# Loads, stores and clears placed differently in a two-layer hybrid decoder: four gate/up buffers, rows out by tile, projections started row tile first

## The chip, the cores and the metric

One Trainium2 chip, one of its cores. The time is the device time of one launch in microseconds, as the median of several runs. Before the change it is 4256.31 us (3 runs, 4256.29 to 4258.72). TensorE (PE) multiplies, VectorE (DVE), ScalarE (ACT) and GpSimd (POOL) do the elementwise work, and SyncE (SP) issues most of the transfers.

## The reference, cut to what matters

1024 tokens of width 1024 go through two layers, all in float32.

```python
for layer in range(2):
    h = rmsnorm(x, norm_mix[layer])
    if layer == 0: x = x + pool_mixer(h, ...)        # windowed means minus the row, four 256x256 matrices, a scale
    else:          x = x + nsa_mixer(h, ...)         # 16 heads, 4 kv heads: compressed, selected and window attention
    h = rmsnorm(x, norm_ffn[layer])
    if layer == 0: x = x + (silu(h @ wg) * (h @ wu)) @ wd    # 1024 -> 3584 -> 1024
    else:          x = x + moe(h, ...)               # router picks 2 of 8 experts of the same shape for each token
    if layer == 0: shared = build_shared_kv(x, ...)  # keys and values of all three branches, from x after layer 0
```

## The kernel before, in words

The kernel is one program of stages, each a block of five instruction streams (one for each engine). A stage has semaphores of its own, which `phase_semaphores` clears at its end, with a barrier of all engines. The stages in order: `pool_mixer`, `swiglu_jobs` for the dense channel mixer ("ffn"), `project_heads` ("kvq"), `compress_keys` ("cmp"), `attend` ("att"), `project_out`, `route`, and `swiglu_jobs` again for the experts ("moe"). Within a stage the order on each engine is the order of the code, and semaphores tie the engines together.

Float32 products are made of three passes: each operand is split into a high part (a cast to the fast 32-bit format, on ACT) and the low rest (a subtraction, on DVE), and PE adds high by high, high by low and low by high.

**`swiglu_jobs`** runs a list of jobs. A job is one expert's weights with up to 384 rows. Its width is one of six (128 to 384), and the jobs run from the widest down. In this data the experts make eight jobs: 384, 352, 320, three of 256, 224 and 128 rows. The dense mixer makes two jobs of 512 rows. A job has MT = 28 gate/up tiles (1 MB of weights each) and NG = 14 down groups (1 MB each). The raw gate/up weights land in two buffers `gu_raw`. ACT makes `gu_hi` of a tile (`split`, L221 to L225), DVE makes `gu_lo` (L306 to L309), and only then may SP load the tile after the next into that buffer (`load_gate_up` waits for `s_gu_lo`, L157). For widths over 128 PE holds the weights still and streams the rows (`gate_up`, L414). For width 128 it is the other way round (`rows_by_weights`, L430), and the hidden rows are transposed behind it (`turn_hidden`, L442). After two tiles comes one down group (`down`, L454), whose sums DVE adds into `yacc` (`add_y`, L335).

At a job's end POOL waits for the last of these sums (L209), copies the row numbers of the job (L2381), issues one adding indirect transfer for each row tile (L2387), pads the count of three with tiny transfers to `spare` (L2391), waits until all have landed (L211), and clears `yacc` for the next job (L204). DVE waits for the clearing (L364) in front of its second tile of the next job. PE transposes the next job's rows before the last down group. They were gathered by POOL (L2373) at the start of the job before. For the first job of the experts nothing precedes: the three gathers are issued while SP already loads gate/up tiles 0 and 1 and down group 0.

**The dense mixer** stores its 512x1024 result `yacc` in one transfer (L2320) after the last sum. **`pool_mixer`** ends with five DVE copies of bias rows out of PSUM (L725) and behind them the last normalised row tile (L699), which SP stores, and then the bias rows (L623).

**`project_heads`** multiplies the eight row tiles by five chunks of 512 columns. ACT does `weight_hi` (L947), `square_x` (L940) and `transposed_x` (L964), and issues the loads of row tiles (`load_x`, L931). DVE does `add_x`, `normed_x`, `low_x`, `weight_lo`. PE transposes row tile i+1 before it multiplies row tile i. Before the change the first four weight slices stand ahead of row tile 0 on ACT and DVE, and `multiply` waits for all eight low slices. **`attend`** begins on SP with the queries of row tile 0 (`load_q`), the keys of tile 0, the constants and values, the queries of tile 1, the keys of tile 1.

## Time and profile before

| what | value |
|---|---|
| median of the runs | 4256.31 us |
| the profiled execution: its own time | 4260.62 us |
| its span, first to last instruction | 4258.1 us |
| mean granted clock of TensorE | 0.969 |
| PE busy | 4030.5 us, 95% |
| DVE busy | 2364.7 us, 56% |
| ACT busy | 1630.4 us, 38% |
| transfers, mean over the span | 139 GB/s |
| gate/up load of 1 MB, issue to landing, median of 226 | 4.8 us |
| granted clock around the first gathers, 2080 to 2101 | 0.53 |

Times in the rows below are microseconds from the start of the span. A matmul's printed duration holds part of its pipeline, so the distance between the starts of two matmuls is the better measure of what one costs. A granted clock of 1.00 is 2.4 GHz, 0.50 is 1.2 GHz.

### The profile page before, as it was taken

How to read it: one execution, taken by the hardware profiler on the slowest of the kernel's cores; microseconds unless marked ns; L12 is line 12 of the kernel's file. 1: busy time of each engine (PE TensorE's matmuls, PEld its weight loads, DVE VectorE, ACT ScalarE, POOL GpSimd, SP SyncE). 2: the span in 40 equal slices, each digit the busy share in tenths (PEclk: the TensorE clock that was granted, in tenths of full speed). 3: DMA queues.
4: the chain of work that ended last, by engine and by line, in shares of the span. 5: the costliest groups of instructions: out<-in, count | busy, mean ns of one | idle time of the engine just before them, and what ended most of it. 6: DMA issues, size and time to landing. Idle time of an engine off the chain costs nothing.

```text
span 4258.1 us, 63421 instructions
## 1 busy us (share of the span) xinstructions
PE 4030.5 (95%) x23002; PEld 3477.4 (82%) x23002; DVE 2364.7 (56%) x3487; ACT 1630.4 (38%) x2255; POOL 425.4 (10%) x433
## 2 busy tenths in 40 slices
PE   7999999997997899998599999999999999999987
PEld 6888888886886555557599999999989999999976
DVE  4444444445443776643455555555566666666677
ACT  3222222222332676672232332333334444444445
POOL 2000000000231243330100010010010101001010
PEclk9999999998998899999699999999999999999998
DMA  5222232223544211005333343344455555555566
GB/s 215 99 100 99 97 128 89 108 99 144 167 137 149 72 43 37 17 18 180 135 132 118 138 151 125 142 153 148 148 175 188 198 190 179 209 185 194 198 239 220
DMA packets 153287, 592.17 MB, mean 139 GB/s; under 512 B 26768, under 2 KB 54800, under 8 KB 112915
## 3 DMA queue, kind: packets, MB, share of 16 engines
q1 hardware_dynamic: 138788, 545.92, 35.6%
q0 software_dynamic: 10288, 35.14, 2.9%
q10 hardware_dynamic: 4080, 9.44, 0.6%
q8 instruction: 73, 1.20, 0.1%
q14 instruction: 58, 0.48, 0.0%
HBM read 533.66 MB, written 57.83 MB: 139 GB/s over the span
## 4 chain that ended last, share of the span: by engine, by line
PE 44%; DMA 3%; DVE 1%; issue 1%; POOL 1%; ACT 1%; POOLq 0%; DVEq 0%; SPq 0%; ACTq 0%
PE moe_ps L424 9%; PE moe_ps L425 9%; PE moe_ps L426 9%; PE moe_ps L466 5%; PE moe_ps L467 5%; PE moe_ps L468 5%; DMA moe_gu_raw<-in_moe_wgu 2%; DVE moe_gu_lo L308 1%; DMA spare<-ident 1%; PE moe_ps L405 1%; ACT moe_gu_hi L225 0%; DMA out_x<-moe_yacc,job_to 0%; POOL moe_yacc L204 0%; DVE moe_yacc L343 0%; DMA moe_stage<-h_moe,moe_ids 0%
## 5 line engine op out<-in xcount | busy, mean ns | idle before, releaser
L424 PE MATMUL moe_ps<-moe_ht_hi,moe_gu_hi 128*128 128x256 f32 (+4 forms) x3136 | 941.5, 300 | 10.2 <-DVE moe_gu_lo L308 8.6
L426 PE MATMUL moe_ps<-moe_ht_hi,moe_gu_lo 128*128 128x256 f32 (+4 forms) x3136 | 940.2, 300 | 0.0
L425 PE MATMUL moe_ps<-moe_ht_lo,moe_gu_hi 128*128 128x256 f32 (+4 forms) x3136 | 939.8, 300 | 0.0
L225 ACT CAST moe_gu_hi<-moe_gu_raw 128x2048 fp32r<-128x2048 f32 x226 | 430.6, 1905 | 553.1 <-PE moe_ps L426 484.4
L308 DVE TENSOR_TENSOR moe_gu_lo<-moe_gu_raw,moe_gu_hi 128x2048 fp32r<-128x2048 f32 x226 | 517.4, 2289 | 183.7 <-ACT moe_gu_hi L225 183.4
L424 PEld LDWEIGHTS moe_ps<-moe_ht_hi,moe_gu_hi 128*128 128x128 f32 x3136 | 599.7, 191 | 14.9 <-DVE moe_gu_lo L308 9.7
L425 PEld LDWEIGHTS moe_ps<-moe_ht_lo,moe_gu_hi 128*128 128x128 f32 x3136 | 600.4, 191 | 3.5
L426 PEld LDWEIGHTS moe_ps<-moe_ht_hi,moe_gu_lo 128*128 128x128 f32 x3136 | 599.3, 191 | 0.0
L343 DVE SCALAR_TENSOR_TENSOR moe_yacc<-moe_ps,job_weights,moe_yacc 128x512 f32<-128x512 f32 x504 | 374.8, 750 | 340.0 <-PE moe_ps L468 340.0
L466 PE MATMUL moe_ps<-moe_wd_hi,moe_hid_hi 128*128 128x512 f32 x1008 | 396.2, 393 | 0.0
L467 PE MATMUL moe_ps<-moe_wd_lo,moe_hid_hi 128*128 128x512 f32 x1008 | 393.9, 391 | 0.0
L468 PE MATMUL moe_ps<-moe_wd_hi,moe_hid_lo 128*128 128x512 f32 x1008 | 393.5, 390 | 0.0
L424 PE MATMUL ffn_ps<-ffn_ht_hi,ffn_gu_hi 128*128 128x512 f32 x896 | 349.9, 391 | 1.9 <-DVE ffn_ht_lo L304 1.9
L426 PE MATMUL ffn_ps<-ffn_ht_hi,ffn_gu_lo 128*128 128x512 f32 x896 | 349.8, 390 | 0.0
L425 PE MATMUL ffn_ps<-ffn_ht_lo,ffn_gu_hi 128*128 128x512 f32 x896 | 349.6, 390 | 0.0
L346 DVE TENSOR_TENSOR ffn_yacc<-ffn_yacc,ffn_ps 128x512 f32<-128x512 f32 x224 | 153.6, 688 | 255.3 <-PE ffn_ps L468 255.0
L250 ACT CAST moe_hid_hi<-moe_hid 128x256 fp32r<-128x256 f32 (+4 forms) x196 | 85.0, 434 | 528.0 <-DVE moe_hid L323 528.0
L333 DVE TENSOR_TENSOR moe_wd_lo<-moe_wd_raw,moe_wd_hi 128x2048 fp32r<-128x2048 f32 x112 | 255.9, 2285 | 0.0
L323 DVE TENSOR_TENSOR moe_hid<-moe_act_gate,moe_ps 128x256 f32<-128x256 f32 (+5 forms) x224 | 96.9, 433 | 285.9 <-PE moe_ps L426 255.7
L468 PEld LDWEIGHTS moe_ps<-moe_wd_hi,moe_hid_lo 128*128 128x128 f32 x1008 | 189.4, 188 | 40.1
L466 PEld LDWEIGHTS moe_ps<-moe_wd_hi,moe_hid_hi 128*128 128x128 f32 x1008 | 190.0, 188 | 37.0 <-DVE moe_yacc L343 1.1
L467 PEld LDWEIGHTS moe_ps<-moe_wd_lo,moe_hid_hi 128*128 128x128 f32 x1008 | 189.7, 188 | 35.5
(355 smaller groups left out, 6490.7 us busy)
## 6 DMA issues: line engine op xcount, KB each, us to landing
moe_gu_raw<-in_moe_wgu SPq DMA_DIRECT2D x226, 1024.0 KB, 4.8
moe_wd_raw<-in_moe_wd SPq DMA_DIRECT2D x112, 1024.0 KB, 6.7
first_gu<-in_ffn_wgu SPq DMA_DIRECT2D x58, 1024.0 KB, 4.8
ffn_wd_raw<-in_ffn_wd SPq DMA_DIRECT2D x28, 1024.0 KB, 6.8
att_qt<-qt SPq DMA_DIRECT2D x8, 1024.0 KB, 4.9
kt<-kt_rows SPq DMA_DIRECT2D x8, 1024.0 KB, 6.9
shared<-in_w_kvq SPq DMA_DIRECT2D x5, 1024.0 KB, 7.8
kvq_raw<-in_w_kvq SPq DMA_DIRECT2D x5, 1024.0 KB, 7.7
```

The costliest lines, as they stand in the source:

```text
L225: act.copy(gu_hi[s][:, :, :, :].rearrange("p a k c -> p (a k c)"), gu_raw[s][:, :]).then_inc(s_gu_hi, 1)
L308: dve.tensor_tensor(gu_lo[s][:, :, :, :].rearrange("p a k c -> p (a k c)"), gu_raw[s][:, :], gu_hi[s][:, :, :, :].rearrange("p a k c -> p ...
L323: dve.tensor_tensor(hid[s][:, 0:W], act_gate[s][:, 0:W], gate_ps[s][:, W:2 * W] if W == P else up_ps[s][:, 0:W], ALU.mult).then_inc(s_hid, 1)
L333: dve.tensor_tensor(wd_lo[b][:, :, :], wd_raw[b][:, :, :], wd_hi[b][:, :, :], ALU.subtract).then_inc(s_wd_lo, 1)
L343: dve.scalar_tensor_tensor(out=part, in0=y_ps[u % 4][:, :], scalar=row_weights[1][:, t:t + 1], in1=part, op0=ALU.mult, op1=ALU.add).then_i ...
L346: dve.tensor_tensor(part, part, y_ps[u % 4][:, :], ALU.add).then_inc(s_yadded, unit)
L424: pe.matmul(out[:, 0:W], gu_hi[s][:, half, k, :], ht_hi[:, k, 0:W], start=(k == 0), stop=False)
L425: pe.matmul(out[:, 0:W], gu_hi[s][:, half, k, :], ht_lo[:, k, 0:W], start=False, stop=False)
L426: last = pe.matmul(out[:, 0:W], gu_lo[s][:, half, k, :], ht_hi[:, k, 0:W], start=False, stop=(k == KT - 1))
L466: pe.matmul(out, hid_hi[b][:, a, rows], wd_hi[b][:, a, cols], start=(a == 0), stop=False)
L467: pe.matmul(out, hid_hi[b][:, a, rows], wd_lo[b][:, a, cols], start=False, stop=False)
L468: last = pe.matmul(out, hid_lo[b][:, a, rows], wd_hi[b][:, a, cols], start=False, stop=(a == GROUP - 1))
```

## The change

It makes these edits; the diff is cut to its core.

- Experts: four gate/up buffers in place of two. The dense mixer keeps two (`RING` is the number). The order of loads on SP stays: one down group, two gate/up tiles, but the tiles are two further ahead.
- Experts' start: SP loads tile 0, waits until the gathered rows of the first job have landed, and only then loads tiles 1 to 3 and the first down group.
- At a job's end POOL copies the row numbers first and waits for the sums of one row tile at a time (`tile_done`), issuing each tile's transfer behind its own wait. The dense mixer stores four transfers of one row tile each in place of one.
- DVE's wait for the cleared `yacc` stands in `add_y`, where `yacc` is used.
- `pool_mixer`: the five copies of bias rows run on ACT, at its end. DVE's last `normed_mid` no longer stands behind them.
- `project_heads`: row tile 0 is squared, normalised and transposed ahead of the weights, `load_x(2)` stands right behind `transposed_x(0)`, the first multiplication is done in two halves with the transposes of row tile 1 between, and `multiply` waits for each weight slice by itself.
- `compress_keys`: SP loads the queries of row tiles 0 and 1 here, into the memory of a buffer that `zrow` no longer needs. `attend` begins with the keys.

```diff
-            stage, gu_raw = sb("stage", [P, CAP, D]), [sb(f"gu_raw{s}", [P, 2 * D]) for s in range(2)]
+            stage, gu_raw = sb("stage", [P, CAP, D]), [sb(f"gu_raw{r}", [P, 2 * D]) for r in range(4)]
...
+        def gu_load_count(j, n, r):
+            return j * (16 // RING * MT) + (n - r) * (16 // RING) + 16
...
-            def load_gate_up(ws, j, n, s):
-                sp.wait_ge(s_gu_lo, j * MT + n + 1)
+            def load_gate_up(ws, j, n, r, first=False):
+                if not first:
+                    sp.wait_ge(s_gu_lo, j * MT + n + (3 - RING))
...
-                for s in range(2):
-                    load_gate_up(first, 0, s, s)
+                load_gate_up(first, 0, 0, 0, first=True)
+                sp.wait_ge(s_rows, 16 * CAP)
+                for r in range(1, RING):
+                    load_gate_up(first, 0, r, r, first=True)
...
-                            load_gate_up(ws, j, it * 4 + (2 * b + 2 + s), s)
+                            load_gate_up(ws, j, it * 4 + (2 * b + RING + s), (2 * b + s) % RING)
+                for q in range(IN_JOB - IN_JOB % 2, NG):
+                    load_down(ws, j, q, q % 2)
+                    if q == IN_JOB:
+                        following = source(j + 1)
+                    for s in range(2):
+                        n = 2 * q + RING + s
+                        load_gate_up(ws if n < MT else following, j, n, n % RING)
...
-                pool.wait_ge(s_yadded, j * 24 * NG + (24 + 24 * NG))
-                put(pool, j, base, yacc, s_stored, per_height)
+                def tile_done(t, tiles):
+                    unit = 12 // tiles
+                    pool.wait_ge(s_yadded, j * 24 * NG + (24 * NG + unit * (2 * t + 2)))
+                    pool.sem_inc(s_store_seen, 1)
+                put(pool, j, base, yacc, s_stored, per_height, tile_done)
...
                     def add_y(q):
+                        dve.wait_ge(s_zeroed, j + 1)
...
                     wdlo(0, 0)
-                    dve.wait_ge(s_zeroed, j + 1)
...
+            for n, (a, b) in enumerate(spans):                       # pool_mixer, ACT, after square_mid(TILES - 1)
+                act.wait_ge(s_vec_mm, n + 1)
+                act.copy(vec[:, a:b], vec_ps[n][0:N_HEADS, 0:b - a]).then_inc(s_vec_made, 1)
...
             load_x(1)                                                # project_heads, ACT
+            square_x(0)
             act.wait_ge(s_gain, 16)
             for k in range(HK):
                 weight_hi(0, k)
-            square_x(0)
+            transposed_x(0)
+            load_x(2)
+            square_x(1)
...
             add_x(0)                                                 # project_heads, DVE
+            normed_x(0)
             dve.wait_ge(s_gain, 16)
             for k in range(HK):
                 weight_lo(0, k)
-            normed_x(0)
+            add_x(1)
+            low_x(0)
+            normed_x(1)
...
             transpose_x(0)                                           # project_heads, PE
-            for n in range(STEPS):
+            multiply(0, half=0)
+            transpose_x(1)
+            multiply(0, half=1)
+            for n in range(1, STEPS):
...
+            for z in range(2):                                       # compress_keys, SP
+                sp.wait_ge(s_tr, (z + 1) * N_KV)
+                load_q(sp, z)
...
-            load_q(0)                                                # attend, SP
             load_keys(0)
...
-            load_q(1)
             load_keys(1)
...
-            pool.dma_start(y_ffn.rearrange("(s p) d -> p s d", p=P)[:, bass.ds(base, DENSE_W // P), :], yacc[:, :, :]).then_inc(s_stored, 16)
+            tiles = DENSE_W // P
+            for t in range(tiles):
+                tile_done(t, tiles)
+                pool.dma_start(y_ffn[bass.ds((base + t) * P, P), :], yacc[:, t, :]).then_inc(s_stored, 16)
...
                 for t in range(tiles):
+                    tile_done(t, tiles)
                     pool.indirect_dma_start(out=out, out_offset=bass.IndirectOffsetOnAxis(ap=job_to[:, t:t + 1], axis=0),
```

## Rows read from the trace of the kernel before

**Rows 1.** Waits of PE over the span: total us, times, longest us.

```profile
PE moe_ps L405 <- DMA moe_stage<-h_moe,moe_ids: 24.3, 1, 24.3
...
PE moe_ps L447 <- DVE moe_hid L323: 19.8, 8, 6.2
...
PE moe_ps L424 <- DVE moe_gu_lo L308: 8.6, 4, 3.8
```

**Rows 2.** Waits in the 128-row job, 4076 to 4243.

```profile
ACT moe_gu_hi L225 <- DMA moe_gu_raw<-in_moe_wgu: 37.8, 21, 4.8
```

**Rows 3.** The 128-row job in time: start, duration, engine, line, operation, idle before.

```profile
4091.82 0.29 DVE L323 TENSOR_TENSOR moe_hid<-moe_act_gate,moe_ps 128x128 f32<-128x128 f32 x1 [4.96 <-POOL moe_yacc L204]
...
4097.06 2.28 DVE L333 TENSOR_TENSOR moe_wd_lo<-moe_wd_raw,moe_wd_hi 128x2048 fp32r<-128x2048 f32 x1
...
4229.18 2.29 DVE L333 TENSOR_TENSOR moe_wd_lo<-moe_wd_raw,moe_wd_hi 128x2048 fp32r<-128x2048 f32 x1
...
4167.58 0.28 PE L433 MATMUL moe_ps<-moe_gu_hi,moe_ht_hi 128*128 128x256 f32 x1
...
4176.48 0.28 PE L433 MATMUL moe_ps<-moe_gu_hi,moe_ht_hi 128*128 128x256 f32 x1
```

**Rows 4.** Stretches: PE, PEld, DVE, ACT, POOL busy; clock; transfers' share; GB/s.

```profile
4125.00:4150.00 25.00, 22.77 (x165) 20.99 (x163) 20.84 (x23) 14.00 (x17) 0.00 (x0) 1.00 0.80 305
...
3125.00:3130.00 5.00, 4.85 (x22) 4.85 (x23) 5.00 (x6) 2.70 (x3) 4.39 (x3) 0.50 0.71 265
...
3858.00:3864.00 6.00, 6.00 (x28) 6.00 (x29) 5.14 (x5) 2.74 (x4) 5.34 (x3) 0.50 0.80 292
```

**Rows 5.** The start of the first 256-row job: PE in time.

```profile
3120.99 0.28 PE L425 MATMUL moe_ps<-moe_ht_lo,moe_gu_hi 128*128 128x256 f32 x1
3121.11 0.28 PE L426 MATMUL moe_ps<-moe_ht_hi,moe_gu_lo 128*128 128x256 f32 x1
...
3125.95 0.42 PE L424 MATMUL moe_ps<-moe_ht_hi,moe_gu_hi 128*128 128x256 f32 x1
3126.16 0.42 PE L425 MATMUL moe_ps<-moe_ht_lo,moe_gu_hi 128*128 128x256 f32 x1
```

**Rows 6.** The first gathers: third one's landing; all gathers; packets of 2078 to 2100 by queue.

```profile
moe_stage<-h_moe,moe_ids POOLq DMA_INDIRECT x1, 12.2
...
DMA to landing us min/median/max: 4.2/9.7/12.9
...
q1 hardware_dynamic: 704, 4.19, 48.2%
q0 software_dynamic: 432, 1.57, 17.6%
```

**Rows 7.** The end of the dense mixer: POOL in time, then a stretch as in rows 4.

```profile
1018.24 0.76 POOL L2320 DMA_DIRECT2D y_ffn<-ffn_yacc  x1 [448.59 <-DVE ffn_yacc L346]
1027.19 0.10 POOL L892 MEMSET kvq_minus_half<- 128x8 f32 x1 [8.20 <-POOLq L41]
...
1020.00:1021.00 1.00, 0.00 (x0) 0.00 (x0) 0.00 (x0) 0.00 (x0) 0.00 (x0) 1.00 1.00 401
```

**Rows 8.** The start of the projections, in time; then the first store's landing.

```profile
1048.74 1.23 DVE L1040 TENSOR_TENSOR first_sum<-first_sum 128x1024 f32<-128x1024 f32 x1 [3.02 <-DMA first_sum<-y_ffn]
...
1040.53 0.34 ACTq L937 DMA_DIRECT2D first_sum<-x_mid  x1
...
x<-first_sum SPq DMA_DIRECT2D x1, 512.0 KB, 9.0
```

**Rows 9.** The start of the attention, in time.

```profile
1369.79 4.44 SPq L1476 DMA_DIRECT2D att_consts<-in_sel_const  x1
...
1378.38 0.75 DVE L1641 TENSOR_TENSOR shared<-att_s,cmpb 128x256 f32<-128x256 f32 x2 [13.45 <-DMA att_valid<-in_row_valid]
```

**Rows 10.** The end of the pool mixer: DVE in time.

```profile
72.12 2.46 DVE L725 COPY pool_vec<-pool_d 16x512 f32<-16x512 f32 x4
```

**Rows 11.** The end of the kernel: POOL in time.

```profile
4246.33 1.63 POOL L2387 DMA_INDIRECT out_x<-moe_yacc,job_to  x1 [1.89 <-issue]
```

More of the change, by code:

```diff
@@ L77, in swiglu_jobs @@
         else:
-            stage, gu_raw = sb("stage", [P, CAP, D]), [sb(f"gu_raw{s}", [P, 2 * D]) for s in range(2)]
-            s_gu_loaded = [sem(f"gu_loaded{s}") for s in range(2)]
+            stage, gu_raw = sb("stage", [P, CAP, D]), [sb(f"gu_raw{r}", [P, 2 * D]) for r in range(4)]
+            s_gu_loaded = [sem(f"gu_loaded{r}") for r in range(4)]
+        RING = len(gu_raw)
+        def gu_load_count(j, n, r):
+            return j * (16 // RING * MT) + (n - r) * (16 // RING) + 16
         ids = sb("ids", [P, CAP], mybir.dt.uint32)
@@ L257, in wdhi, with post_and_split @@
                         act.copy(wd_hi[b][:, :, :], wd_raw[b][:, :, :]).then_inc(s_wd_hi, 1)
-                    def post_and_split(m, q, s, b, first=False):
+                    def post_and_split(m, q, s, b, r, first=False):
                         silu(j * MT + m, s)
@@ L346, in add_y, with post_and_split @@
                                 dve.tensor_tensor(part, part, y_ps[u % 4][:, :], ALU.add).then_inc(s_yadded, unit)
-                    def post_and_split(m, s, b, first=False):
+                    def post_and_split(m, s, b, r, first=False):
                         product(j * MT + m, s)
@@ L1160, in transpose_x, with multiply @@
                 last.then_inc(s_t, 1)
-            def multiply(n):
+            def multiply(n, half=None):
                 c, i = divmod(n, TILES)
@@ L1171, in multiply @@
                 at_rows = slice(i * P, (i + 1) * P)
-                for k in range(KT):
+                for k in range(KT) if half is None else range(half * HK, half * HK + HK):
+                    if i == 0:
+                        pe.wait_ge(s_wlo, c * KT + k + 1)
                     pe.matmul(acc[n % 4][:, :], xt_hi[:, k, at_rows], w_hi[c % 2][:, k, :], start=(k == 0), stop=False)
@@ L1176, in multiply @@
                                      start=False, stop=(k == KT - 1))
-                last.then_inc(s_mm, 1)
+                if half != 0:
+                    last.then_inc(s_mm, 1)
             def transpose_heads(n):
@@ L1218, in _, with compress_keys @@
                 transpose_gates(half)
-def compress_keys(nc, zrow, first_w1, pos, w1, w2, kc_gain, ident, kct, vc):
+def compress_keys(nc, zrow, first_w1, pos, w1, w2, kc_gain, ident, kct, vc, load_q):
     NBL = 64
@@ L1402, in attend @@
         vs, vw = first_sum[:, :].rearrange("p (i n) -> p i n", i=TILES), sb("vw", [P, TILES, N_KV * DH])
-        qt = [sb(f"qt{s}", [P, N_HEADS, P], F32R) for s in range(2)]
         p_slc = [sb(f"p_slc{s}", [P, R, SEQ]) for s in range(2)]
@@ L1421, in attend @@
         o_ps = [ctx.enter_context(nc.psum_tensor(f"att_o{s}", [P, 512], F32)) for s in range(2)]
-        s_const, s_qt = sem("const"), [sem(f"qt{s}") for s in range(2)]
+        s_const = sem("const")
         s_kt, s_values = [sem(f"kt{s}") for s in range(2)], sem("values")
@@ L2331, in trunk, with load_q @@
             vc = sb(att, "vc", [P // 2, N_KV, DH])
+            w_lo1 = sb(att, "kvq_lo1", [P, KT, 512], F32R)
+            qt = [w_lo1[:, 4 * s:4 * s + 4, :].rearrange("p a (b t) -> p (a b) t", t=P) for s in range(2)]
+            s_q = [nc.alloc_semaphore(f"queries{s}") for s in range(2)]
+            def load_q(sp, i):
+                sp.dma_start(qt[i % 2].bitcast(F32), qt_dram[i * P:(i + 1) * P, :].rearrange("p (h t) -> p h t", t=P)
+                             ).then_inc(s_q[i % 2], 16)
             with ExitStack() as early:
                 raw = [shared[:, :].rearrange("p (k n) -> p k n", k=KT // 2), sb(early, "kvq_raw", [P, KT // 2, 512])[:, :, :]]
-                w_lo1 = sb(early, "kvq_lo1", [P, KT, 512], F32R)
                 zrow = [w_lo1[:, 4 * z:4 * z + 4, :].bitcast(F32).rearrange("p m (g l d) -> p m g l d", g=N_KV, l=2) for z in range(2)]
```

118 lines of the change are left out of this document (56 added, 62 removed).

## The prediction, written before the result was known

> **What bounds the kernel now.** I read the share of busy time first: PE works 95% of the span, so only what ends PE's idle time, or its time at half clock, can pay. The list of PE's waits [rows 1] then says where that is: 24.3 us for the first gathered expert rows, 19.8 us in the 128-row job for hidden rows that DVE makes late, 8.6 us at four job starts for `gu_lo`. The other places are the seams between stages, where PE waits for a new stage's first data. The reader is to see that all edits are at such places. In the long middle of every wide job PE has no wait, and nothing there changes.
>
> One stage is not bound by PE's own work: the last job, 128 rows wide. Its ACT waits 37.8 us for gate/up transfers in 21 pieces [rows 2]. From the second to the fourteenth low part of a down group it takes 4229.18 - 4097.06 = 132.1 us [rows 3], 12 steps of 11.01 us. A step is a pair of gate/up tiles and a down group. PE does one in 4176.48 - 4167.58 = 8.90 us where nothing holds it [rows 3]. DVE is busy 20.84 of 25 us there [rows 4], 0.83 of 11.01, so 9.2 us. PE and DVE are almost equal, and the transfers at 305 GB/s have 0.80 of the engines' time [rows 4]. A step moves three loads, 3.15 MB. At the 401 GB/s that a full stretch shows [rows 7] that is 7.8 us.
>
> **The sum, part by part,** against the profiled execution's own 4260.6 us, which is 4.3 us over the median. I subtract the same number from the median.
>
> *Four gate/up buffers.* Before, a tile's raw load may only start when the low part of the tile two before is made, and ACT then waits for its landing. With four, the load starts two tiles (some 9 us) earlier against the page's median of 4.8 us to land, so those 37.8 us go. What is late next is PE or DVE: the step is no shorter than 8.90, and DVE's 9.2 is a sum of durations that overlap a little. I take 9.2 us. 12 x (11.01 - 9.2) = 21.7 us. Bounds: 12 x (11.01 - 8.90) = 25.3 us, and 0 if transfers or SP's order keep the step. In wider jobs the buffers hide nothing: there PE waits for no load.
>
> *Clearing awaited at use.* DVE's second tile of a job waited for `yacc`. In the 128-row job that is 4.96 us [rows 3], and all behind it on DVE (the low parts of tile 3 and of down group 1) follows, so 4.9 us. In the three 256-row jobs and the 224-row job PE's waits for `gu_lo` [rows 1] go, 8.6 us. Two of these were long enough to be followed by half clock: 5 us behind 3125 and 6 us behind 3858 [rows 4]. A 256-column matmul starts every 0.12 us at full clock and every 0.21 at half [rows 5], so of 11 us some 0.43 is lost, 4.8 us. Together 18.3 us. The new wait is in front of the first `add_y`. It stands behind four gate/up tiles and a down group, over 25 us into the wide jobs. In the narrow one these are 4 x 3 + 2.7 us plus the start's waits, some 17 us from 4076, and the clearing was over at 4091.8, 15.7 us in [rows 3], with copying ahead making it 2 us earlier. So I cost it at nothing, with 3 us of cover. If that were gone, DVE's next splits would queue behind the wait, and PE behind them, each us one to one. That the cleared memory is written beside DVE's work costs nothing new, since POOL already issued such clears beside DVE.
>
> *Rows awaited before more weights.* The third gather took 12.2 us to land while 4.19 MB of weights moved beside 1.57 MB of rows [rows 6]. After the change only tile 0 (1.05 MB) competes, and 2.6 MB take 6.5 us from 2080.5, to 2087. The quickest gather of all landed in 4.2 us [rows 6], which from 2083.2 is 2087.4. I take that: 8.0 us. The bound on the low side is the median landing of 9.7 us: 2.5 us. Nothing waits behind SP's held queue: tile 1 is wanted 8 us after PE begins, and one load takes 4.8 us. The down group comes fourth, some 12 us after the rows, against 11 us plus 6.4 us of transposes before ACT asks for it. The Trainium skill (DMA: Bandwidth & Descriptors, Queues, rings and completion order) says that each transfer engine turns between its queues packet by packet. By that rule the 432 row packets would have met 432 of the 704 weight packets, 2.57 MB, and 4.1 MB at 401 GB/s put the landing near 2091, not 2095.4. The gain would be nearer 4 us, as part of the landing is then the gather's own. The trace does not agree fully, as the rows came last.
>
> *Stores by tile.* The dense result leaves in one 2 MB transfer issued at 1018.24, and the next stage starts at 1027.19 [rows 7]. The last tile alone is 0.5 MB, so three quarters of 5.2 us at 401 GB/s move ahead, under the last sums: 3.8 us, bounds 3.0 and 4.2. At a job's end in the experts each output transfer goes out earlier, hidden by PE's next tiles. Only at the kernel's end is it on the path, and there only because the row numbers are copied ahead of the wait: 1.89 us of issue [rows 11] become some 0.3. That is 1.8 us with the copy.
>
> *Projections.* Row tile 2's load was issued at 1040.53, landed for the sum at 1048.74, and from there each row tile takes 7.0 us, the time of its load and sum, to the end of the chunk. So the whole chunk moves with this load. After the change its issue waits for the first store, which landed 9.0 us behind its issue at 1029.3 [rows 8], so 1038.3, 2.2 us earlier. It then also has less traffic beside it (the second half of chunk 1 is issued later). I put its sum 4.0 us earlier. Bounds: 2.2, and 5.0 where it lands like the later ones, in 5.4 us.
>
> *Attention.* DVE's first work waits 13.45 us, to 1378.38, for the last small constant. The issue of the constants alone held SP for 4.44 us [rows 9], behind queries and keys. Without the queries in front, the keys' 1 MB lands 2.6 us sooner at 401 GB/s, or, if the queue stays held as long, only the 0.7 us of their issue is won. I take 2.5. In `compress_keys` the two query loads lie beside one weight load that is wanted 15 us later. They cost nothing, and if they delayed it, each us would count one to one.
>
> *Pool mixer.* Four copies take 2.46 us on DVE from 72.12 [rows 10], with the fifth 2.9 us in front of the last row tile. On ACT, idle there, they end at the same time or slightly later, and the last tile no longer follows them: 1.7 us of 1.3 to 1.9.
>
> *What it adds.* DVE's wait in each `add_y`, PE's per-slice waits, POOL's wait and count per tile: some 300 instructions, hidden but in the 128-row job and at the end. I take 1 us.
>
> Sum: 21.7 + 18.3 + 8.0 + 3.8 + 1.8 + 4.0 + 2.5 + 1.7 - 1.0 = 60.8 us. The profile would read 4199.8, the median **4195.5**.
>
> **The rivals.** *The narrow job stays at its transfers' pace.* SP still issues in one fixed order, and 0.80 of the transfer engines' time is used already. If latency under a fuller queue or SP's place in the order holds, the step stays near 11 us. The job then gains only the clearing, and the time is 4256.3 - 39.1 = 4217.2. Against it: the landings are under 8 us and would have 17. In between lie half gains, about 4206.
>
> *The gathers are slow by themselves.* The median of 27 gathers is 9.7 us [rows 6], though nearly all had weights beside them. Then 5.5 us are missing: 4201. By the Trainium skill's rule above (same section) it would be about 4199.
>
> *Half clock in the narrow job (the slower side).* Half clock followed waits of 3.76 and 2.4 us and not those of 1.1 and 1.3. If PE, once ahead of DVE, stood over 2.5 us in every step, a step would run at half clock. 48 matmuls of 256 columns cost 10.1 us instead of 5.8, and the rest doubles from 3.1, so about 16.3 us a step. 12 x (16.3 - 11.01) = 63 us more, and the time is 4256.3 - 39.1 + 63 = 4281. It decides from 15 us a step on (39.1 + 8.5 us over 12 steps, on top of 11.01). Against it: the stretch ran at 1.00 even with the transfer waits [rows 4], and these waits go.
>
> *The change doesn't do what it says* in one seam: a stage's first data lands late for another reason, say keys or the first stored row. Each is 2 to 4 us.
>
> **How the numbers follow.** The forecast with its seams as priced, narrow step 8.9 to 9.7 us: 0.62, with a range of its own of 4187 to 4205. The narrow job at its old pace or half way: 0.24, 4205 to 4221. Gathers slow or two seams failing with the narrow job right: 0.09, within 4198 to 4210. Half clock, or another loss over the whole gain: 0.03. Better than all bounds: 0.02. The range for 8 in 10 is 4186 to 4218: it takes in the best bounds (another 3.6 + 0.9 + 0.4 + 1.0 us, and some tail) and the old pace. A measurement of this kernel tells about 0.2%, 8.5 us, from no change. Faster by more: 0.95. Within it: 0.02. Slower: 0.03.
>
> **What would show it.** In the 128-row job ACT's waits for `moe_gu_raw` are near nothing and `moe_wd_lo` starts every 9.2 us. PE has no wait for `moe_gu_lo` at job starts, and no half clock at the first 256-row and the 224-row job. The first expert transposes start about 7 us after the first gather is issued instead of 15. The dense mixer's last issue and the next stage's first instruction are 5 us apart instead of 9. In the projections the first sum of row tile 2 comes 17 to 18 us into the stage, not 21.6. DVE's first work in the attention comes 7.4 us into the stage instead of 9.95. Wrong would be: a step still at 11 us with waits on DMA (first rival), a new wait of DVE for POOL's clearing in front of `add_y`, or w1 of the compression landing after PE wants it.

## The result, and the profile after

The changed kernel takes **4197.4 us** (median of 4 runs, 4194.9 to 4201.7) against 4256.3 before. The ratio is 0.9861, with a 95% interval of 0.9849 to 0.9874. The forecast was 4195.5, with 4186 to 4218 as its range. The profiled execution took 4201.67 us (span 4200.1, granted clock 0.973), so between the two profiled executions lie 58.0 us of span, where the sum had 60.8.

I cut both spans at the first instruction of each stage and read what each term became. Seams are measured as in the last part of the prediction.

| term of the sum | forecast | before to after, from rows | measured |
|---|---|---|---|
| four gate/up buffers | 21.7 | 12 steps of the narrow job: 132.1 to 110.7 | 21.4 |
| clearing awaited at use | 18.3 | jobs 3 to 7: 15.3 shorter; narrow job up to its second `wd_lo`: 20.2 to 15.2 | 20.3 |
| rows before more weights | 8.0 | experts' start to first `ht_hi`: 17.0 to 10.5 | 6.4 |
| stores by tile | 3.8 | last dense addition to next stage: 10.4 to 6.8 | 3.6 |
| tail | 1.8 | last `wd_lo` to the end: 28.9 to 27.4 | 1.5 |
| projections | 4.0 | stage: 295.0 to 293.8 | 1.2 |
| attention's first work | 2.5 | 9.9 to 6.9 | 3.1 |
| pool mixer | 1.7 | last scale to next stage: 9.45 to 7.75 | 1.7 |
| instructions added | -1.0 | nothing seen | 0 |
| elsewhere | 0 | pool mixer 1.9 shorter; dense mixer 2.1 longer, compression 0.1 longer, attention from its first work to the experts' start 0.9 longer | -1.3 |

The measured column gives 57.9. The row "elsewhere" is no effect of the change (last section).

PE's list of waits in the changed kernel, the answer to [rows 1] (line waited at, by whom, us in total, times, longest):

```profile
PE moe_ps L424 <- DMA moe_stage<-h_moe,moe_ids: 17.9, 1, 17.9
PE kvq_t L1186 <- DVE first_sum L1067: 16.7, 4, 11.3
...
PE moe_ps L466 <- DVE moe_hid L342: 4.7, 4, 1.6
```

24.3 became 17.9, 19.8 became 4.7 (the turning of hidden rows, now L466), and of the four waits for `gu_lo` 0.2 us are left. The projections' wait shows that a seam is left there.

The narrow job, low parts of down groups two, three and fourteen on DVE, the answer to [rows 3], and the windows (busy us of PE, PEld, DVE, ACT and POOL, then granted clock, DMA share, GB/s), the answer to [rows 4]:

```profile
4062.07 2.29 DVE L352 TENSOR_TENSOR moe_wd_lo<-moe_wd_raw,moe_wd_hi 128x2048 fp32r<-128x2048 f32 x1
4071.25 2.29 DVE L352 TENSOR_TENSOR moe_wd_lo<-moe_wd_raw,moe_wd_hi 128x2048 fp32r<-128x2048 f32 x1
...
4172.77 2.29 DVE L352 TENSOR_TENSOR moe_wd_lo<-moe_wd_raw,moe_wd_hi 128x2048 fp32r<-128x2048 f32 x1
```

```profile
4120.00:4145.00 25.00, 25.00 (x182) 23.39 (x181) 24.37 (x27) 17.01 (x21) 0.00 (x0) 1.00 0.90 340
```

(4172.77 - 4062.07) / 12 = 9.23 us a step. DVE is busy 24.37 of 25 us, so it is the bound, as forecast. The transfers went from 0.80 to 0.90 of the engines' time without holding anything. In this job ACT has no wait for a gate/up load any more.

The experts' start on POOL and PE (third gather's issue, first transposes), the answer to [rows 6], and the seam behind the dense mixer on POOL, the answer to [rows 7]:

```profile
2074.97 0.94 POOL L2412 DMA_INDIRECT moe_stage<-h_moe,moe_ids  x1 [0.30 <-issue]
```

```profile
2080.78 4.75 PE L424 MATMUL moe_ps<-ident,moe_stage 128*128 128x128 f32 x24 [17.92 <-DMA moe_stage<-h_moe,moe_ids]
```

```profile
1016.85 0.53 POOL L2352 DMA_DIRECT2D y_ffn<-ffn_yacc  x1 [2.18 <-DVE ffn_yacc L367]
1022.19 0.10 POOL L911 MEMSET kvq_minus_half<- 128x8 f32 x1 [4.81 <-POOLq L41]
```

The third gather lands 5.8 us behind its issue, not the forecast's 4.2. The last 0.5 MB store takes 5.3 us to the next stage's first instruction, where 2 MB took 8.95.

The projections on ACT and its queue (loads of row tiles 2 and 3, squares of tiles 1 and 2), and on DVE two low parts of weights and the sums, the answer to [rows 8]:

```profile
1032.65 0.33 ACTq L956 DMA_DIRECT2D first_sum<-x_mid  x1
1033.02 1.00 ACTq L957 DMA_DIRECT2D first_sum<-y_ffn  x1
1034.06 1.06 ACT L964 ACTIVATE kvq_work<-kvq_work 128x1024 f32<-128x1024 f32 x1 [4.52 <-issue]
...
1042.16 1.06 ACT L964 ACTIVATE first_sum<-first_sum 128x1024 f32<-128x1024 f32 x1 [3.27 <-DVE first_sum L1063]
1042.25 0.33 ACTq L956 DMA_DIRECT2D kvq_work<-x_mid  x1
```

```profile
1039.59 1.41 DVE L1076 SCALAR_TENSOR_TENSOR kvq_lo<-shared,kvq_gains,kvq_hi 128x512 fp32r<-128x512 f32 x2
1040.91 1.22 DVE L1063 TENSOR_TENSOR first_sum<-first_sum 128x1024 f32<-128x1024 f32 x1
...
1049.33 1.23 DVE L1063 TENSOR_TENSOR kvq_work<-kvq_work 128x1024 f32<-128x1024 f32 x1 [1.70 <-DMA kvq_work<-y_ffn]
```

The stage starts at 1022.19. Row tile 2's sum comes 18.7 us in (21.55 before, forecast 17 to 18), but tile 3's comes 8.4 us later, where it was 7.1 before: of 2.8 us only 1.5 are left there.

The second half of tile 2's load, from issue to landing (the last number, us), before and then after; it was issued at 1040.90 and at 1033.02:

```profile
first_sum<-y_ffn ACTq DMA_DIRECT2D x1, 512.0 KB, 7.8
```

```profile
first_sum<-y_ffn ACTq DMA_DIRECT2D x1, 512.0 KB, 6.6
```

So it landed 21.5 us into the stage before and 17.4 after, 4.1 us earlier. Its sum did not follow at once: it stands behind the low weight parts in DVE's order, which end at 1041.0.

### The profile page after: what moved, and what is told of

Read it like the earlier page. It is cut to its first block, busy times and chain, and to the rows that moved or that the text cites. A ratio compares the mean times of both kernels' runs of the same rounds, so it can differ in the third digit from the quotient of the medians.

```text
span 4200.1 us, 63442 instructions
## 1 busy us (share of the span) xinstructions
PE 4015.1 (96%) x23002; PEld 3464.3 (82%) x23002; DVE 2363.0 (56%) x3482; ACT 1631.3 (39%) x2260; POOL 423.9 (10%) x439
## 4 chain that ended last, share of the span: by engine, by line
PE 49%; DVE 1%; issue 0%; ACT 0%; DMA 0%; POOL 0%; DVEq 0%; POOLq 0%; ACTq 0%
PE moe_ps L443 10%; PE moe_ps L445 10%; PE moe_ps L444 10%; PE moe_ps L485 5%; PE moe_ps L486 5%; PE moe_ps L487 5%; PE moe_ps L424 1%; PE moe_ps L452 1%; PE moe_ps L453 1%; PE moe_ps L456 1%; DVE moe_yacc L364 0%; DMA moe_stage<-h_moe,moe_ids 0%; DVE moe_ht_lo L323 0%; PE moe_ps L458 0%; DVE moe_wd_lo L352 0%
## 5 line engine op out<-in xcount | busy, mean ns | idle before, releaser
L2427 POOL DMA_INDIRECT out_x<-moe_yacc,job_to x18 | 28.8, 1597 | 1955.1 <-DVE moe_yacc L364 1955.1
```

## The experiments

A stage whose code is unchanged repeats closely: the 352-row job took 334.53 to 334.57 us in every kernel, the second 256-row job 241.97 to 242.03 wherever nothing stalled it. So small effects are read from their own stage, and the medians (they spread by 2 to 7 us) only where an effect is larger.

### Two buffers

```diff
-[sb(f"gu_raw{r}", [P, 2 * D]) for r in range(4)]
+[sb(f"gu_raw{r}", [P, 2 * D]) for r in range(2)]
```

> The changed kernel with two gate/up buffers in the experts instead of four, all else kept. The prediction's theory (the 128-row job waits for loads that start only when the low part of the tile two before is made): the step of that job goes from 9.2 us back to 11.0, ACT waits again some 30 to 38 us for gate/up transfers, and the median is 4197.4 + 21.7 = 4219, nothing else moving. Rival (the loads were late because of the clearing and the start, and the step would have shortened with two buffers too): the step stays under 9.7 us and the median is within 6 us of 4197.

Measured: **4219.05 us**. The expert stage is 2151.3 us long against 2128.9, that is 22.4 more, and nearly all of it lies in the narrow job. ACT's waits from 2430 us on:

```profile
ACT moe_gu_hi L244 <- DMA moe_gu_raw<-in_moe_wgu: 47.3, 24, 5.0
```

The second to fourteenth `wd_lo` are 130.2 us apart, 10.85 a step. So 19.5 us lie in the 12 steps and 2.5 ahead of the second `wd_lo` (17.7 us into the job, 15.2 in the changed kernel). The other jobs change by 0.1 us at most. The rival is out: the four buffers are worth what the sum said.

### The clearing: five runs

The two edits are the place of DVE's wait and the moment of the expert stores:

```diff
 def add_y(q):
-    dve.wait_ge(s_zeroed, j + 1)
...
 wdlo(0, 0)
+dve.wait_ge(s_zeroed, j + 1)
```

```diff
 for t in range(tiles):
     tile_done(t, tiles)
+for t in range(tiles):
     pool.indirect_dma_start(out=out, ...)
```

> The changed kernel with DVE's wait for the cleared accumulator put back in front of the second tile of a job; stores by tile stay. The prediction's theory (the place of this wait is worth 18.3 us): 4197.4 + 18.3 = 4215.7, PE's waits for the low gate/up parts are back at four job starts and DVE waits some 5 us in the 128-row job. Rival (what the trace after suggests: storing tile by tile already ends the clearing 11.2 us into the 128-row job instead of 14.7, so it is 3.5 us earlier, and the old waits were 5.0, 3.8, 2.4, 1.3 and 1.1 us): only some 1.4 us in the narrow job and 0.3 us elsewhere come back, no half clock, and the median is 4198 to 4201.

> The changed kernel with the expert outputs stored only when all tiles of the job are summed, as before; the wait for the clearing stays at its use. The prediction costed storing by tile in the experts at nothing but the tail (which has one tile in the last job, so it keeps its copy ahead). Both theories: the clearing ends some 3.5 us later, 14 to 15 us into the 128-row job, while the first addition there comes 17.4 us in, so 2.7 us of cover are left and the median stays within 2 us of 4197.4. If the cover were less than thought, DVE would wait in front of its first addition and the time grow one to one.

> The changed kernel with both undone: stores of the expert outputs at the job's end, and the wait for the clearing in front of the second tile. Theory of the prediction: 18.3 us are lost, as in the run with the wait alone, 4215.7. Rival (either of the two edits alone buys nearly all of it): the waits of before are back only here, 4214 to 4216, while each alone is within 4 us of 4197.4. The theories differ not in this run but in how it stands to the two before it.

Measured: 4202.3, 4198.2 and **4210.0 us**. In the stage itself: with the wait back alone jobs 3 to 7 are as in the changed kernel within 0.05 us, with the stores at the end too; the narrow job is 0.5 us longer in the one, 0.9 shorter in the other. Only with both back do jobs 4 to 7 lose 6.3 us and the narrow job 2.3. DVE's waits for the clearing, from 2430 us on, with the wait back alone and with both back:

```profile
DVE moe_hid L342 <- POOL moe_yacc L219: 0.7, 2, 0.4
```

```profile
DVE moe_hid L342 <- POOL moe_yacc L219: 20.4, 7, 4.5
```

The first run's median is 4.9 us over that of the changed kernel and just outside the rival's 4198 to 4201, but the expert stage has only 0.3 us of it, and its profiled execution (4199.8) is no longer than the changed kernel's (4201.7). So the rival holds: either edit alone buys nearly all. But both back cost only 8.4 us of the stage, not 20, and 4210.0 lies under both theories of that run. The next run asks for the rest.

```diff
-pool.tensor_copy(job_to...)          # ahead of the waits for the sums
 for t in range(tiles):
     tile_done(t, tiles)
+pool.tensor_copy(job_to...)          # behind them
```

> As the run with both back (stores of expert outputs at the job's end, the wait for the clearing in front of the second tile), and the row numbers copied behind the last sum, not ahead of it. That is the clearing of before with four gate/up buffers. Stages of these kernels repeat within 0.1 us from run to run, so I read the expert stage alone, from the first clearing to the end of the span: 2121.5 us in the changed kernel, 2129.9 with both back. Theory now (the copy ahead is the third cause: it ends each clearing 1.1 us earlier, and the stall falls on both sides of the clock's drop): the stage takes 2121.5 + 20.2 + 0.3 = 2142, the jobs of 256, 256, 256 and 224 rows last 249.2, 243.4, 242.6 and 236.6 us again. Rival (the copy is worth nothing but its 0.3 to 1.9 us at the kernel's end; the rest of the difference came with the four buffers): 2131 to 2132.

Measured: **4213.6 us**, the expert stage 2143.0, which is 14.1 more than the changed kernel: between the theory (20.5) and the rival (9.5 to 10.5). The four jobs lasted 247.1, 242.4, 242.5 and 234.5, cut as in the expectation. That cut puts the end of the first two 0.9 us behind the last addition, at DVE's copy of the row weights; cut at the last addition they lasted 246.2, 242.4, 243.4 and 234.5 (before: 248.3, 243.4, 243.5, 236.6), which is the cut from here on. One reason was open: do four buffers absorb a part, or is the clearing not as late as it was?

> Two gate/up buffers and the clearing of before together (stores at the job's end, row numbers copied behind the last sum, the wait in front of the second tile); all other edits of the change stay. The expert stage, from its first instruction to the end of the span, took 2128.9 us in the changed kernel, 22.4 more with two buffers alone, 14.1 more with the clearing of before alone. Theory A (the two causes are separate, as the prediction's sum took them): 2128.9 + 22.4 + 14.1 = 2165.4, and the jobs of 256, 256, 256 and 224 rows last 247.1, 242.4, 242.5 and 234.5 us as in the run with the clearing of before alone. Theory B (with four buffers the tiles behind the stalled one are already in memory, so the ring absorbs part of what a late clearing costs; the kernel before, 2178.7 less the 6.4 us that its rows came later, points there): 2172, the four jobs last 249.2, 243.4, 242.6 and 236.6 us, and the median is some 4240.

Measured: **4233.3 us**, the expert stage 2163.9. The two causes add (22.4 + 14.1 = 36.5 against 35.0), so theory A holds for the sum: the ring absorbs nothing. Job by job it is mixed. The first 256-row job lost 6.6 us, where A took 4.2 over from the run before it, but its clearing also ended 17.5 us in, not 15.9; jobs 6 and 7 lost 2.7 us less than there. What is left is seen when each job's loss is put beside the time at which its clearing ended, counted from the end of the last addition of the job before (both from POOL's and DVE's rows; the loss is against the changed kernel):

| kernel | job 5 (256 rows) | job 6 (256) | job 7 (224) |
|---|---|---|---|
| wait back, stores by tile | 10.7: 0.0 | 10.9: 0.0 | 11.2: 0.0 |
| both back | 13.5: 0.3 | 13.5: 0.3 | 13.6: 1.6 |
| both and the copy back | 13.6: 0.4 | 14.5: 1.4 | 14.1: 3.7 |
| the same with two buffers | 13.5: 0.3 | 13.4: 0.2 | 14.1: 2.1 |
| before | 14.6: 1.4 | 14.7: 1.5 | 14.7: 5.7 |

One rule, read off these rows and tested by no further run, fits all five kernels within 0.1 us: with the wait in front of the second tile, a 256-row job loses what its clearing ends past 13.2 us, and a 224-row job what it ends past 12.0, and more where half clock follows. In the last column 14.1 stands with 3.7 and with 2.1. PE waited 1.85 and 1.80 us, and the windows behind the wait show half clock for a part of the time in the first and not in the second (the granted clock is the third number from the end):

```profile
3836.00:3840.00 4.00, 2.45 (x12) 2.45 (x13) 4.00 (x4) 3.75 (x4) 3.70 (x2) 0.73 0.30 68
3840.00:3844.00 4.00, 4.00 (x33) 4.00 (x32) 2.80 (x3) 0.67 (x2) 3.31 (x2) 0.84 1.00 413
```

```profile
3835.00:3839.00 4.00, 2.93 (x26) 2.93 (x27) 4.00 (x5) 3.58 (x3) 3.70 (x2) 1.00 0.43 115
3839.00:3843.00 4.00, 4.00 (x32) 3.73 (x31) 2.32 (x2) 1.63 (x2) 2.83 (x2) 1.00 1.01 407
```

My rebuilt clearing is still earlier than that of before, because I left the read of the job's height ahead of the waits. POOL's first output transfer starts 1.1 us behind the copy there, and 1.8 us in the kernel before. So the runs give back 14.1 of the clearing's 20.3 us; the other 6 rest on the rule above and on no run. These rows are of the run with the copy back and of before:

```profile
3820.82 0.18 POOL L2423 COPY job_to<-slot_to 128x3 uint32 x1 [219.67 <-DVE moe_yacc L362]
3821.94 1.63 POOL L2427 DMA_INDIRECT out_x<-moe_yacc,job_to  x1 [0.94 <-POOL job_to L2423]
```

```profile
3840.48 0.18 POOL L2381 COPY job_to<-slot_to 128x3 uint32 x1 [219.73 <-DVE moe_yacc L343]
3842.31 1.63 POOL L2387 DMA_INDIRECT out_x<-moe_yacc,job_to  x1 [1.65 <-issue]
```

### The first rows of the experts: two runs

```diff
 load_gate_up(first, 0, 0, 0, first=True)
-sp.wait_ge(s_rows, 16 * CAP)
 for r in range(1, RING):
```

> The changed kernel without SP's wait for the gathered rows at the experts' start: all four gate/up loads and the first down group, 5.2 MB, are issued at once beside the three gathers. Theory by volume (the rows land when what was issued with them has moved, as the trace of before seemed to say): 6.8 MB at some 380 GB/s from 2071 on, the third gather lands 14 to 16 us behind its issue, and the first transposes start 17 to 19 us behind the first gather's issue, against 14.9 in the kernel before and 8.5 in the changed one; 8 to 10 us lost. Rival (queues take turns, so that only as many weight packets as row packets are in the way): the landing does not depend on how much is queued behind, it is again 12.2 us, the transposes start 15 us behind the first gather, and 6.4 us are lost.

```diff
-load_gate_up(first, 0, 0, 0, first=True)
 sp.wait_ge(s_rows, 16 * CAP)
-for r in range(1, RING):
+for r in range(RING):
```

> The changed kernel with the first gate/up tile of the experts too held until the gathered rows have landed, so that the three gathers have the transfer engines to themselves. In the changed kernel the third gather landed 5.8 us behind its issue with 1.05 MB of weights beside it. Theory of the prediction (a gather by itself lands in 4.2 us, the rest is traffic): the transposes start 1.6 us earlier; the first tile then lands 4.8 us behind the rows, its two parts take 4.2 us, and PE starts its first gate sum 9 us behind the rows instead of some 7, so the stage loses 0.5 to 1.5 us in all. Rival (the gathers are slow by themselves): they land in 5.8 us again, and the stage loses 2.5 to 3.5 us.

PE's first transposes with the loads at once and with the rows alone; the third gathers were issued at 2069.24 and 2064.67:

```profile
2082.82 4.53 PE L423 MATMUL moe_ps<-ident,moe_stage 128*128 128x128 f32 x24 [25.68 <-DMA moe_stage<-h_moe,moe_ids]
```

```profile
2070.08 2.82 PE L423 MATMUL moe_ps<-ident,moe_stage 128*128 128x128 f32 x12 [17.52 <-DMA moe_stage<-h_moe,moe_ids]
2079.71 2.82 PE L423 MATMUL moe_ps<-ident,moe_stage 128*128 128x128 f32 x12 [6.81 <-DVE moe_ht_lo L322]
```

The landing of the third gather is thus 5.4 us by itself, 5.8 with one weight load beside it, 12.2 in the kernel before and 13.6 with all at once. (The 5.4 is one execution. In the eleven kernels that start the experts as the changed one does, itself among them, PE's first transpose starts 5.5 to 6.4 us behind that issue.) The forecast's 4.2 was the quickest of 27 gathers, and these do not reach it. Both kernels lost about 8 us of the expert stage (2136.8 and 2136.7 against 2128.9).

The first loss, 7.9, lies near the theory's 8 to 10, but the theory's reason does not hold: the rows did not come last. These are the packets, MB and shares of the two queues (q1 weights, q0 rows) from the first row packet to the last, before (2084.94 to 2094.90) and with all at once (2070.97 to 2082.28), and then with all at once behind the rows' landing (2082.82 to 2088.00):

```profile
q1 hardware_dynamic: 475, 2.58, 62.9%
q0 software_dynamic: 432, 1.57, 39.0%
```

```profile
q1 hardware_dynamic: 501, 3.16, 67.1%
q0 software_dynamic: 432, 1.57, 34.3%
```

```profile
q1 hardware_dynamic: 230, 1.34, 62.8%
```

The 432 row packets met 475 weight packets in the one kernel and 501 in the other, nearly one for one, and 1.34 MB of the queued weights moved only behind them. So the queues took turns, as the rival had it. What the rival left out is that the weight packets held more, 3.16 MB and not 2.58: together they moved at 419 and 418 GB/s, and the rows took 11.3 us and not 9.9, which is all of the difference between 13.6 and 12.2. By the Trainium skill (DMA: Bandwidth & Descriptors, Queues, rings and completion order) each transfer engine turns between its queues a packet at a time. The packet counts here agree with that.

The second run refuted my expectation for another reason. ACT and DVE take tile 0 ahead of the transposed rows in their order. With tile 0 late, the rows landed early and then stood 6.8 us until DVE was through with `gu_lo` at 2079.2. Tile 0 in front, as the change has it, costs the gathers 0.4 us (5.8 against 5.4) and saves this.

### The projections: two runs, and the seams

```diff
 if i:
-    if i + 1 < TILES: square_x(i + 1)
     transposed_x(i)
 if 0 < i < TILES - 2: load_x(i + 2)
+if i and i + 1 < TILES: square_x(i + 1)
```

> The changed kernel with one more order: in the projections' first chunk ACT issues the load of row tile i+2 ahead of the square of row tile i+1, not behind it. Theory (the trace after: the load of tile i+2 goes out 0.1 us after the square of tile i+1 starts, lands 5.3 to 7.1 us later, and this loop of load and sum sets 7.0 us a tile, while PE needs 6.35): the tiles come every 6.3 to 6.5 us, and the time from the stage's start to the last sum of the chunk, 72.3 us now and 73.8 before, becomes 67 to 69; the whole gains 3 to 5 us. Rival 1 (the store of the tile whose buffer is reused lands late and holds the issue, and with it ACT and the next square): the tiles still come every 7 us and nothing is gained, or up to 2 us are lost. Rival 2 (the load's landing is stretched by the chunk's weights whatever its issue): under 1.5 us are gained.

Measured: **4194.7 us**. The last sum of the chunk comes 70.0 us into the stage (72.3), not the 67 to 69 of the theory, and the stage takes 290.9 us (293.8). Half of the theory holds. Tile 3's load now goes out 3.5 us earlier and its sum is made 24.3 us into the stage, not 27.1; the load had landed at 21.6, and the sum stands behind other work in DVE's order. But tile 4's load stands behind the copy of tile 2's transposes (ACT at 1047.13, after 3.3 us of waiting for PE), and its issue holds ACT and the next square for another 1.5 us, much as the first rival said. What it waits for there is the store of the tile whose buffer it takes. That store, the first line below with its us from issue to landing, was issued at 1042.11 and so landed at 1048.6:

```profile
x<-first_sum SPq DMA_DIRECT2D x1, 512.0 KB, 6.5
```

```profile
1048.66 0.33 ACTq L956 DMA_DIRECT2D first_sum<-x_mid  x1
1049.02 0.56 ACTq L957 DMA_DIRECT2D first_sum<-y_ffn  x1
1049.69 1.06 ACT L964 ACTIVATE kvq_work<-kvq_work 128x1024 f32<-128x1024 f32 x1 [1.54 <-issue]
```

The opposite test puts the old order back on ACT, DVE and PE (ACT's part of the edit):

```diff
-square_x(0)
 act.wait_ge(s_gain, 16)
 for k in range(HK): weight_hi(0, k)
-transposed_x(0); load_x(2); square_x(1)
+square_x(0)
```

> The changed kernel with the projections' orders on ACT, DVE and PE as before (weights of the first chunk ahead of the row tiles). The prediction gave the new order 4.0 us. Its theory: from the stage's start to the last sum of the first chunk 72.3 + 4.0 = 76.3 us, and the stage as a whole 4 us longer. Rival (what the two traces show: row tile 2's load goes out 2.9 us earlier, but row tile 3's load then lands 1.4 us later behind its issue, and half of the gain is given back): 73.8 us to the last sum as in the kernel before, and the stage 295.0 us instead of 293.8, so 1.2 to 1.5 us.

Measured: 4196.9 us. The last sum comes 73.3 us in, the stage takes 294.4 us. Ten kernels with the new order have 292.5 to 293.9 (mean 293.2), the two with the old one 295.0 and 294.4. The new order is worth 1.5 us, not 4.0.

The other seams went back together, as they lie in different stages (short: `load_q` at the attention's start, one 2 MB `dma_start` in `dense_store`, the five copies of `vec` on DVE, four of them of full width):

> The changed kernel with three seams as before: the queries are loaded by the attention itself (queries 0 ahead of the keys, queries 1 ahead of the next keys), the dense mixer stores its result in one 2 MB transfer, and the four copies of the bias rows are on DVE in front of the pool mixer's last row tile. Each lies in a stage of its own and is read there. Theory (each edit is worth what the trace after shows at its seam): from the dense mixer's last addition to the next stage's first instruction 10.4 us instead of 6.8; from the last scale of the pool mixer to the next stage 9.4 us instead of 7.7; DVE's first work in the attention 9.9 us into the stage instead of 6.9. Together 8.3 us, a median of 4205 to 4206. Rival for the attention (the keys and constants, not the queries, set the landing; the gain of before to after was a quieter queue): DVE's first work stays under 8 us into the stage. Rival for the store (its landing is mostly the transfer's own latency): under 8 us at that seam.

Measured: **4205.9 us**. POOL's rows of that kernel at the end of the pool mixer and of the dense mixer:

```profile
72.30 0.19 POOL L531 TENSOR_SCALAR pool_rs_mid<-pool_ss_mid 128x1 f32<-128x1 f32 x1 [2.77 <-ACT pool_squares L673]
...
81.76 0.95 POOL L207 MEMSET ffn_hid_hi<- 128x1024 f32 x1 [8.63 <-POOLq L41]
```

```profile
1018.23 0.76 POOL L2349 DMA_DIRECT2D y_ffn<-ffn_yacc  x1 [448.58 <-DVE ffn_yacc L367]
1027.20 0.10 POOL L911 MEMSET kvq_minus_half<- 128x8 f32 x1 [8.21 <-POOLq L41]
```

9.46 us (7.75), 10.47 us from the last addition (6.78), and 9.5 us to DVE's first work in the attention (6.9). All three theories hold within 0.4 us. At DVE's first reduction in the attention 0.9 us are left of the 2.6 (12.5 us in, 11.6 in the changed kernel, 14.7 before), since here a part of PE's first scores ran at full clock: the granted clock was 0.66 from 1366.9 to 1380 and 0.50 from 1362 to 1375 in the changed kernel. The issue of the constants held SP for 3.50 us with the queries ahead and 1.99 without.

### A version that beats both

```diff
-load_keys(0)
-sp.dma_start(consts[:, :, :], sel_const).then_inc(s_const, 16)
 sp.dma_start(valid[:, :], row_valid).then_inc(s_const, 16)
+sp.dma_start(consts[:, :, :], sel_const).then_inc(s_const, 16)
+load_keys(0)
```

The edit also has ACT's order of the run with loads ahead.

> A version that should beat both: the changed kernel with the loads of the row tiles issued ahead of the next square (as in the run with loads ahead, 2.3 us less in that stage), and in the attention the two small constants loaded ahead of the keys. The latter: DVE's first work there waits for the small constant that is issued 2.7 us into the stage, behind 1 MB of keys, and lands 4.2 us later. Theory (it shares the transfer engines with the keys): ahead of them it lands 2 to 2.5 us behind an issue 0.5 to 2.5 us into the stage, DVE starts 4.5 to 5 us in instead of 6.9, and the whole takes 4197.4 - 2.3 - 2.2 = 4193. Rival (the landing of some 4 us is that transfer's own, or the other constant's issue holds it): DVE starts 6.2 us in or later, and only 0 to 0.7 us are won: 4194.5. Against it too: the keys are then issued 2.4 us later, and if PE wanted them, each us would be lost one to one; it wants them 10.8 us into the stage.

Measured: **4190.6 us** (4189.7 to 4191.9), against 4194.9 to 4201.7 of the changed kernel. They did not run on the same chip. The ratio to before is 0.9851 (0.9835 to 0.9868), so the medians alone do not separate it from the changed kernel's 0.9861. The stages do. SP, DVE and PE at the attention's start, which begins at 1357.99:

```profile
1358.37 0.43 SPq L1506 DMA_DIRECT2D att_consts<-in_sel_const  x1
```

```profile
1360.63 0.42 DVE L1670 TENSOR_TENSOR shared<-att_s,cmpb 128x256 f32<-128x256 f32 x1 [6.15 <-DMA att_consts<-in_sel_const]
```

```profile
1365.44 0.63 PE L1805 MATMUL att_s<-kt,kvq_lo 128*128 128x128 f32 x4 [1.01 <-DMA kt<-kt_rows]
```

DVE starts 2.6 us in, not 6.9, and PE then waits 1.0 us for the keys. DVE's first reduction comes 6.9 us in instead of 11.6: 4.7 us won where I expected 2.2. The projections took 292.4 us here, so against the mean of 293.2 loads ahead were worth 0.8 us in this run and 2.3 in the other. The second half of tile 3's load, issued ahead in both, took 8.6 us to land here and 4.7 there.

## Why the prediction was right, step by step

The sum came out 1.9 us over the measured 58.9, and some of that closeness is luck: the single terms are off by up to 2.8 us, both ways, and "elsewhere" is chance. The two large terms were right in size.

**Four buffers (21.7): right in mechanism and size**, shown by taking them away (22.4) and by taking away the clearing too (22.4 + 14.1 against 35.0). The 21.4 of the 12 steps is less well shown: both kernels with two buffers put back need 130.1 to 130.2 us for them, not 132.1. DVE is the bound that was named, at 9.23 us a step where 9.2 was forecast.

**Clearing (18.3): right in sum (20.3), wrong in cause.** The failing step is that the stores by tile were "hidden by PE's next tiles", and "copying ahead making it 2 us earlier" counted only as cover, so that both were costed at nothing but the tail and the new place of the wait got the whole. What sets the loss is when the clearing ends against where DVE waits. Stores by tile and the copy end it 10 to 11.2 us into the jobs of 256 rows and fewer, where the old place of the wait needs it at 13.2 or 12.0, so they alone remove the stall. The new place of the wait alone does too. They are substitutes: putting either back leaves the wide jobs as they are and makes the narrow one 0.5 us longer or 0.9 shorter. The cover in the narrow job was right: with the stores at the end the clearing ends 13.6 us in and the first addition comes 17.3 in, and no wait appears.

**Rows (8.0): 6.4.** The term was mis-sized by the landing of a gather without traffic, 5.4 us and not 4.2. That is part of the second rival (gathers slow by themselves), but far from its 9.7. The forecast of transposes about 7 us behind the first gather was 8.5, and with the rows alone it was still 8.1. The prediction's reading that "the rows came last" was wrong as well. By the rule of turns it had 2.57 MB of weights beside the rows, and the trace has 2.58; it came to 2091 only because it counted from the first issue at 2080.5, while the first row packet moved at 2084.9. From there 4.15 MB at 418 GB/s end at 2094.9.

**Stores by tile (3.8: 3.6), tail (1.8: 1.5), pool mixer (1.7: 1.7), attention (2.5: 3.1):** shown by the three seams put back (3.7, 1.7 and 2.6 us), except for the tail. From the end of the last addition to the end of the span, 13.98 us became 12.75, so 1.2 us are the tail's own. The run with the copy behind the last sum, but the read of the job's height still ahead of it, has 13.41.

**Projections (4.0: 1.2, and 1.5 over all kernels): the term that failed.** Its step was "So the whole chunk moves with this load". The load itself did what was forecast: it went out 2.9 us earlier (2.2 forecast) and landed 4.1 us earlier (4.0 forecast for its sum). Then 1.3 us went in DVE's order, where the sum of tile 2 stands behind the low weight parts, and 1.3 us with the next load, which is tied to the next square and led to its sum 7.1 us behind its issue, not 5.8. I did not look at where each later load and sum stand in the orders of ACT and DVE.

**Rivals.** The step at 11 us and the half clock in the narrow job did not come: the clock was 1.00 in its windows from 4047 to 4167. The 1.0 us for added instructions is not found anywhere.

## What to carry to other kernels

Before pricing a stall by its wait, ask what ends it and when: two edits that each move one side past the other are substitutes, and a sum that gives one of them the whole is right only while both stay. A load that lands earlier moves a chain only as far as the next load in the ring and the order of the engine that uses it let it. In a queue of small and large transfers at a stage's start, what the first instruction waits for belongs in front, even if it is a few kilobytes.

## What the hardware showed that I had not expected

The same code behind the same wait runs at two speeds. At 13.6 us in the pool mixer PE resumes after 1.1 us, in both kernels. Before, pairs of products then start every 0.43 us for 3.9 us, after every 0.22, though the granted clock reads 1.00 in the windows from 14 to 18 us of both:

```profile
14.62 0.64 PE L737 MATMUL pool_d<-pool_band,pool_xh 128*128 128x128 f32 x2
15.05 0.64 PE L740 MATMUL pool_d<-pool_band,pool_xh 128*128 128x128 f32 x2
```

```profile
14.12 0.39 PE L756 MATMUL pool_d<-pool_band,pool_xh 128*128 128x128 f32 x2
14.34 0.39 PE L759 MATMUL pool_d<-pool_band,pool_xh 128*128 128x128 f32 x2
```

The pool mixer takes one of two times: 78.3 to 78.6 us in seven kernels, 80.0 to 80.6 in five with the same code. In the seven PE needs 3.65 us from this resuming to its first `pool_y` product, in the five 5.2 to 5.9 us. The dense mixer needs 934.2 to 934.3 us from its stage's start to its last addition in ten of these kernels and 937.1 in two, the changed one among them. In these two the granted clock is still 0.50 some 10 to 12 us into the stage, where it is 1.00 in the others (windows of the run with the stores at the end, whose stage starts at the same time, then of the changed kernel):

```profile
88.00:90.00 2.00, 1.30 (x6) 1.08 (x7) 0.89 (x2) 1.98 (x2) 1.15 (x2) 1.00 0.00 0
```

```profile
88.00:90.00 2.00, 1.36 (x3) 1.17 (x4) 0.89 (x2) 1.98 (x2) 1.21 (x2) 0.50 0.00 0
```

The compression took 46.0 to 47.1 us, and 48.7 and 48.8 in two kernels. From the attention's start to the experts' (attention, output projection, routing) it is 702 to 709 us in eleven kernels with the same code there. What differs in the compression and in this stretch stays open. One profiled execution thus carries some 2 to 3 us of chance in each of three stages and up to 7 in the fourth stretch, which is why terms under 2 us were read at their own seams.
